# The rotary part of the last attention's logits: a contraction over 64 rows in place of 128

## The reference, cut to what matters

```python
MLA_HEADS, MLA_QK_NOPE, MLA_QK_ROPE, MLA_V_DIM = 16, 128, 64, 128

def mla_attention(h, pos, w_dq, cq_norm, w_uq, q_nope_norm, q_pe_norm, w_o, k_nope, k_pe, v):
    c_q = rms_norm_2(h @ w_dq, cq_norm)
    q = (c_q @ w_uq).reshape(b, s, MLA_HEADS, MLA_QK_NOPE + MLA_QK_ROPE)
    q_nope = rms_norm_2(q[..., :MLA_QK_NOPE], q_nope_norm)
    q_pe = rotary(rms_norm_2(q[..., MLA_QK_NOPE:], q_pe_norm), pos)
    ...
    def block(args):                      # 128 queries at a time
        i, qn, qp = args
        sc = (jnp.einsum('bqhd,bkhd->bhqk', qn, k_nope)
              + jnp.einsum('bqhr,bkr->bhqk', qp, k_pe)).astype(jnp.float32) * scale
        sc = jnp.where(causal_mask(i, s), sc, NEG_INF)
        a = jax.nn.softmax(sc, axis=-1)
        return jnp.einsum('bhqk,bkhv->bqhv', a.astype(v.dtype), v)
    ...
```

## Time and profile before

| | |
|---|---|
| median of 3 runs | 3387.99 us (3381.89 to 3389.69) |
| the profiled execution's own time | 3379.43 us |
| its span, first to last instruction | 3377.5 us |
| TensorE busy (matmuls) | 3072.3 us, 91% of the span |
| TensorE busy (weight loads, beside the matmuls) | 2278.2 us |
| VectorE, ScalarE, GpSimd busy | 1399.3, 937.3, 1292.2 us |
| mean granted clock of TensorE | 0.945 of full speed |
| the last attention, first L2229 to last L2251 | from 2555.2 us to about 2838 us |

### The profile page before, as it was taken

How to read it: one execution, slowest core, us unless ns; L and a number is a source line. 1 busy time by engine, 2 the same in 40 slices (tenths; PEclk the granted TensorE clock), 3 DMA queues, 4 the chain that set the end, 5 groups by cost and what they waited for, 6 DMA issues and landing times.

```text
span 3377.5 us, 38890 instructions
## 1 busy us (share of the span) xinstructions
PE 3072.3 (91%) x12698; PEld 2278.2 (67%) x12698; DVE 1399.3 (41%) x2309; ACT 937.3 (28%) x1617; POOL 1292.2 (38%) x631
## 2 busy tenths in 40 slices
PE   6999989886798999987888889999779999899998
PEld 2688856663486688865555568887546677688886
DVE  6211243883234311245322355542643544455425
ACT  3211022333312211023333323320334552233202
POOL 0455443220154555444222245554441112455544
PEclk9999989898999999998878899999889999999999
DMA  4222321110032222321111122232211111222232
GB/s 160 74 93 92 92 72 57 50 62 19 13 106 87 65 95 93 92 72 62 53 53 54 40 88 98 92 90 84 83 56 42 38 32 51 80 93 93 89 92 94
DMA packets 78588, 249.14 MB, mean 74 GB/s; under 512 B 9072, under 2 KB 15728, under 8 KB 78384
## 3 DMA queue, kind: packets, MB, share of 16 engines
q1 hardware_dynamic: 64800, 229.74, 21.1%
q10 hardware_dynamic: 13712, 18.44, 1.7%
HBM read 238.57 MB, written 9.44 MB: 73 GB/s over the span
## 4 chain that ended last, share of the span: by engine, by line
PE 83%; DVE 8%; ACT 4%; issue 2%; POOL 1%; DMA 1%; ACTq 0%; DVEq 0%; POOLq 0%; SPq 0%
PE ps L297 23%; PE ps L298 23%; PE ps L299 23%; DVE tmp L493 2%; PE ps L1926 2%; PE ps L1895 1%; PE ps L2210 1%; PE ps L2251 1%; PE ps L2229 1%; PE ps L2230 1%; PE ps L1293 1%; PE ps L1116 1%; POOL xl L481 1%; PE ps L452 1%; PE ps L1868 1%
## 5 line engine op out<-in xcount | busy, mean ns | idle before, releaser
L291 POOL TENSOR_TENSOR w_lo<-raw,w_hi 128x1024 fp32r<-128x1024 f32 (+1 forms) x438 | 1038.9, 2372 | 1463.3 <-DVE w_hi L284 1463.3
L297 PE MATMUL ps<-xh,w_hi 128*128 128x512 f32 x2248 | 912.5, 406 | 59.2 <-DVE xl L481 34.3
L298 PE MATMUL ps<-xl,w_hi 128*128 128x512 f32 x2248 | 895.1, 398 | 0.0
L299 PE MATMUL ps<-xh,w_lo 128*128 128x512 f32 x2248 | 894.5, 398 | 0.0
L284 DVE CAST w_hi<-raw 128x1024 fp32r<-128x1024 f32 (+1 forms) x438 | 330.1, 754 | 1338.3 <-PE ps L299 1319.5
L297 PEld LDWEIGHTS ps<-xh,w_hi 128*128 128x128 f32 x2248 | 425.4, 189 | 202.4 <-issue 52.6
L298 PEld LDWEIGHTS ps<-xl,w_hi 128*128 128x128 f32 x2248 | 426.8, 190 | 104.0 <-issue 4.8
L299 PEld LDWEIGHTS ps<-xh,w_lo 128*128 128x128 f32 x2248 | 425.9, 189 | 104.7
L297 PE MATMUL ps<-ah,w_hi 128*128 128x512 f32 x704 | 278.1, 395 | 0.0
L298 PE MATMUL ps<-al,w_hi 128*128 128x512 f32 x704 | 278.1, 395 | 0.0
L299 PE MATMUL ps<-ah,w_lo 128*128 128x512 f32 x704 | 278.1, 395 | 0.0
(11 more groups left out here) (360 smaller groups left out, 3722.1 us busy)
## 6 DMA issues: line engine op xcount, KB each, us to landing
raw<-in_ffn_up SPq DMA_DIRECT2D x90, 512.0 KB, 3.5
raw<-in_conv_up SPq DMA_DIRECT2D x88, 512.0 KB, 3.5
raw<-in_ffn_down SPq DMA_DIRECT2D x32, 512.0 KB, 3.5
raw<-in_conv_down SPq DMA_DIRECT2D x32, 512.0 KB, 3.5
raw<-in_merge SPq DMA_DIRECT2D x24, 512.0 KB, 3.6
raw<-in_ple_gate SPq DMA_DIRECT2D x24, 512.0 KB, 4.4
raw<-in_diff SPq DMA_DIRECT2D x24, 512.0 KB, 3.5
raw<-in_mla SPq DMA_DIRECT2D x20, 512.0 KB, 3.5
```

Of the source, the lines that this page charges most:

```text
L291: pool.tensor_tensor(self.w_lo[s][:, 0:n], self.raw[r][:, 0:n], self.w_hi[s][:, 0:n].bitcast(F32), ALU.subtract).then_inc(self.sem["slot_s ...
L297: pe.matmul(out, wh, xh, start=start, stop=False)
L298: pe.matmul(out, wh, xl, start=False, stop=False)
L299: return pe.matmul(out, wl, xh, start=False, stop=stop)
```

## The change

Line 2230 contracts over 64 rows, those in which head j of the pair has its rotary numbers, in place of all 128. The same slice is taken of the queries (the stationary side) and of the keys (the moving side). The rows that hold zeros are no longer read by it; they are still written.

```diff
         bank, n = k.ps[:, u % 2, :], P * (b + 1)
         pe.matmul(bank[:, 0:n], k.mq[:, r % 2, j, b * P:n], k.mk[:, r % 2, j, 0:n], start=True, stop=False)
-        pe.matmul(bank[:, 0:n], k.qpe[:, r % 2, b * P:n], k.kpe[:, j, 0:n], start=False, stop=False)
+        own = slice(64 * j, 64 * j + 64)
+        pe.matmul(bank[:, 0:n], k.qpe[own, r % 2, b * P:n], k.kpe[own, j, 0:n], start=False, stop=False)
         pe.matmul(bank[:, b * P:n], k.ident_b, k.causal_b, start=False, stop=True).then_inc(k.sem["logits"], 1)
```

## The result

The changed kernel takes 3405.27 us (median of 6 runs, 3399.12 to 3407.61), against 3388.84 us for the kernel before (6 runs, 3381.89 to 3391.44). The ratio is 1.0048, 95% interval 1.0035 to 1.0061: 16.4 us slower, and by the interval between 12 and 21 us. The predicted time was 3405.

What follows compares the result with a forecast made beforehand. TensorE's in-order queue was taken to bound the kernel. Streaming 0 plus 19.3 us of round trips, less 2.4 swallowed by waits, gave 16.9, rounded to +17, on 3388.0: 3405 us, range 3396 to 3413.

Steps and rivals of the forecast that it cites:

- TensorE's queue bounds the stage: In the last attention TensorE's in-order queue sets the time; only some 8 of 285 us are waits.
- Term 1: At L2230, streaming time goes by columns whatever the number of rows, so the change there is 0.
- Term 2: Last attention: going from 128 rows to 64 and back costs 0.30 us a unit, 19.3 us in all.
- Term 3: Existing TensorE waits in the last attention swallow 2.4 us: 0.9 rotated queries, 0.9 sum of squares, 0.6 tail.
- The clock: Rival: the clock also falls in the last attention's tail, adding some 9 us, to 3414 us; chance 7%.
- Half the rows, half the time: Rival: L2230 occupies the array half as long, 17 us less, 3371 us; chance 5%.
- Free switch: Rival: changing rows at L2230 costs nothing, DiffHeads' surplus having another cause; time 3388 us; chance 8%.

Runs made afterwards that it cites:

- e3: Changed kernel with each unit's rotary matmul cut in two by columns and the 128-row mask between the halves: 3420.1 us (ratio 1.0096).
- e5: Kernel before with the rotary matmul L2230 deleted: 3361.1 us (ratio 0.9917).
- e1: Changed kernel with the 64-row matmuls of two units issued one behind the other, 32 round trips instead of 64: 3419.5 us (ratio 1.0103).
- e7: The changed kernel run once more, on the same chip as e5 and e6: 3401.9 us (ratio 1.0043 to the kernel before).
- e6: Kernel before with the reverse change in DiffHeads, its 64-row logits matmuls made 128 rows deep by zero-padded keys: 3354.6 us (ratio 0.9903).
- e8: e6 with a small 64-row, 128-column matmul over the zero rows behind each DiffHeads logits matmul: 3367.6 us (ratio 0.9958).
- e4: Same column cut as e3, mask between the halves, but with all 128 rows, as its control: 3392.2 us (ratio 1.0009).
- e9: e6 with TensorE's two waits at the third unit of DiffHeads moved behind that unit's logits: 3355.4 us (ratio 0.9909).
- e10: e6 run once more, beside e9 on the same chip: 3353.4 us (ratio 0.9899).

## Why the prediction was right, point by point

- *TensorE's queue bounds the stage.* Shown: 15.9 us of growth in the stage for 0.30 us in nearly every one of 64 units, and the time moves both ways with this queue in e3 and e5, though in e5 by 26 us for 33 taken out.
- *Term 1, streaming 0.* Right: least, median and longest record are 272, 482 and 693 ns for 275, 453 and 593. All of the growth is in the constant.
- *Term 2, 0.30 a round trip.* Right. I set the 64 units of the two timelines beside each other, start of L2229 to start of what follows the mask. 512 keys go from 1.77 to 2.07 us, 384 from 1.35 to 1.65, 256 from 0.92 to 1.22, 128 from 0.48 to 0.77. Unit 0, at the low clock, grows by 0.42 (predicted 0.38). DiffHeads, read by the two neighbours of its 64-row matmul, was the right twin. Fewer (e1) and more (e3) round trips showed that the price belongs to the trip and neither to the matmul nor to its columns. The Trainium skill's rule, in "TensorEngine Tiling (Array Packing)", section Key Properties, is that a change of the tiling mode, not just of the tile, drains TensorE. The traces agree, at 0.30 us a round trip, and in e1 the second matmul in the same mode pays nothing (records of 1.02 us, as at full depth).
- *Term 3, what waits swallow.* Right in its three parts: 0.9 us at the rotated queries (units 16, 32, 48), 0.9 at the sum of squares (the units 12, 28 and 44 grow by 0.01 or 0.02 only), 0.6 in the tail (units 56 and 60 do not grow). Not foreseen: units 5, 21, 37 and 53 grow by 0.18 and not by 0.30, because a pause of some 0.1 us stood behind their mask; 0.5 us together. And 0.3 us went behind unit 0, where the profile of the change leaves the low clock two matmuls earlier. The 64 units themselves grow by 17.4 us together, the time between them shrinks by 1.5 (0.9 at the rotated queries, 0.3 behind unit 0, the rest in hundredths), and 17.4 - 1.5 is the 15.9 of the stage.
- *The number.* The mechanism and the 17 us were earned. That the median came within 1 us of 3405 is luck as well: single runs of one kernel spread over 9 us, and a second set of runs, e7, gave 3401.9.
- *The clock.* It stayed at 0.99 in the stage, as forecast. Its price, 9 us for 10 us of work at half speed, should have been 10. And one argument against that rival was weak: I took the 1.00 of IdxScore as a sign that 64-row work does not lower the clock. e6 and e8 show that with 128 rows DiffHeads holds 0.93 and 0.95 where it had 0.80. That the last attention was spared because most of its work is 128 rows deep is my reading; no run shows it.
- *Half the rows, half the time*: fell, since the longest record of L2231 is 693 ns and not some 300. *Free switch*: fell, by the 0.30 us a unit.

## What to carry to other kernels

Contracting over 64 rows in place of 128 did not shorten the matmul; between full-depth neighbours it cost a constant instead (0.30 us here at the full clock), with no weight load under the matmul before it at either change. Zeros in the unused rows of one operand were cheaper in both stages tried, and where a stage alternates between 64 and 128 rows padding is worth a try: in DiffHeads it gave 1.0% of the whole kernel, round trips and clock together. Look at the weight loads: a load that starts with its own matmul, behind an idle loader with nothing awaited, is the sign.

## What the runs showed of the hardware that I had not expected

In DiffHeads the granted clock went with the depth of the work: the same matmuls, in the same order, had 0.80 of full speed with 64 rows and 0.93 with 128, and 0.95 with 128 although the 64 changes of rows were put back. It is not depth alone: in IdxScore, without any neighbour of another depth, 64-row matmuls had the full clock from 572 to 578 us (0.85 in the 6 us before). Why the two stages differ stays open.

The clock is not the same in every profile of a stage with the same code, either. The last attention began at the low clock in the profiles of the kernel before and of the change, and at the full one in those of e4, e6, e8, e9 and e10, which is worth 2.6 to 2.8 us; in the last four it is a gain outside of DiffHeads. So the stage is better compared from its third unit on. From the start of the third unit to the start of the last it is 255.3 us in the kernel before and again in e6, e8 and e10, 270.6 in both profiles of the change (15.3 more), and 258.0 in e4 (2.7 more, for the 3 that were expected).
